# Attention steps of a two-layer diffusion step: the exponential read twice out of PSUM in place of a copy

## What is computed

```python
def one(qblk):
    s = jnp.einsum('bqhd,bkhd->bhqk', qblk, k, preferred_element_type=F32) * scale
    p = jax.nn.softmax(s, axis=-1).astype(v.dtype)
    return jnp.einsum('bhqk,bkhd->bqhd', p, v)
```

## Time and profile before

| | |
|---|---|
| median of 3 runs | 3153.99 us (3151.72 to 3156.88) |
| profiled execution: time | 3155.11 us |
| profiled execution: span from first to last instruction | 3153.0 us |
| mean granted TensorE clock over the span | 0.968 of full |
| PE busy in the span | 3011.7 us, 96% |
| ACT busy, DVE busy, POOL busy | 1001.6 us, 1491.0 us, 904.0 us |

### The profile page before, as it was taken

The page is one execution under the profiler, slowest core; times in us unless marked ns, Lnnn a source line. Parts: engine busy times, 40 slices in busy tenths (PEclk is TensorE's granted clock), DMA queues, the critical chain, the costliest instruction groups (busy, mean ns, idle before and its releaser), DMA issues.

```text
span 3153.0 us, 43418 instructions
## 1 busy us (share of the span) xinstructions
PE 3011.7 (96%) x17065; PEld 2884.9 (91%) x17065; DVE 1491.0 (47%) x1825; ACT 1001.6 (32%) x1439; POOL 904.0 (29%) x573
## 2 busy tenths in 40 slices
PE   7999998999999999888999999998989999999999
PEld 7999998999999999787778888786989999999999
DVE  8445546456445554744566655566442222222222
ACT  3111213111111122323777677776222111121111
POOL 0221121112212121122665556666212112222111
PEclk7999998999999999897999999999989999999999
DMA  5222220222212221120000000000201111111112
GB/s 202 96 80 80 80 100 27 81 80 81 70 61 80 80 73 60 53 82 6 8 7 7 2 7 5 8 7 1 100 27 47 41 40 40 47 40 41 40 45 80
DMA packets 45539, 166.69 MB, mean 53 GB/s; under 512 B 5793, under 2 KB 7457, under 8 KB 45217
## 3 DMA queue, kind: packets, MB, share of 16 engines
q1 hardware_dynamic: 44912, 160.89, 15.0%
q10 hardware_dynamic: 560, 4.87, 0.4%
HBM read 156.15 MB, written 9.58 MB: 53 GB/s over the span
## 4 chain that ended last, share of the span: by engine, by line
PE 53%; issue 30%; POOL 14%; DVE 2%; ACT 1%; POOLq 0%; DVEq 0%; ACTq 0%
PE ps L907 52%; POOL p_lo L505 10%; POOL w_lo L489 2%; DVE x L1466 0%; POOL rot L516 0%; POOL q_tok L520 0%; DVE ps L1382 0%; POOL rot L514 0%; PE ps L1002 0%; PE ps L1212 0%; ACT tmp L592 0%; PE ps L996 0%; DVE tmp L1406 0%; POOLq L504 0%; DVE sums L1801 0%
## 5 line engine op out<-in xcount | busy, mean ns | idle before, releaser
L489 POOL TENSOR_TENSOR w_lo<-w_raw,w_hi 128x1024 fp32r<-128x1024 f32 (+2 forms) x190 | 465.2, 2449 | 1884.3 <-ACT w_hi L585 1884.3
L907 PE MATMUL ps<-h_hi,w_hi 128*128 128x384 f32 x2640 | 606.8, 337 | 37.7 <-DVE h_lo L1447 20.2
L907 PE MATMUL ps<-h_lo,w_hi 128*128 128x384 f32 x2640 | 603.3, 336 | 0.0
L907 PE MATMUL ps<-h_hi,w_lo 128*128 128x384 f32 x2640 | 602.6, 336 | 0.0
L907 PEld LDWEIGHTS ps<-h_hi,w_hi 128*128 128x128 f32 x2640 | 473.7, 190 | 42.4 <-issue 29.8
L585 ACT ACTIVATE w_hi<-w_raw 128x1024 fp32r<-128x1024 f32 (+2 forms) x190 | 194.7, 1025 | 956.7 <-PE ps L907 860.9
L907 PEld LDWEIGHTS ps<-h_lo,w_hi 128*128 128x128 f32 x2640 | 474.3, 189 | 0.0
L907 PEld LDWEIGHTS ps<-h_hi,w_lo 128*128 128x128 f32 x2640 | 473.6, 189 | 0.0
L505 POOL TENSOR_TENSOR p_lo<-p,p_hi 128x512 fp32r<-128x512 f32 (+1 forms) x304 | 389.8, 1294 | 257.2 <-ACT p_hi L830 253.3
L1466 DVE SCALAR_TENSOR_TENSOR x<-ps,mod,x 128x256 f32<-128x256 f32 (+5 forms) x432 | 240.2, 612 | 457.9 <-PE ps L907 456.9
L907 PE MATMUL ps<-hid_hi,w_hi 128*128 128x384 f32 x1536 | 348.8, 334 | 0.5 <-DVE x L1466 0.5
(11 more groups left out here) (142 smaller groups left out, 3551.4 us busy)
## 6 DMA issues: line engine op xcount, KB each, us to landing
w_raw<-in_wall_dram SPq DMA_DIRECT2D x174, 512.0 KB, 3.7
mod_raw<-in_mod_rows_dram SPq DMA_DIRECT2D x80, 512.0 KB, 3.6
x<-in_x_t_dram SPq DMA_DIRECT2D x8, 576.0 KB, 8.4
x_spill<-x ACTq DMA_DIRECT2D x1, 4608.0 KB, 13.8
x<-x_spill SPq DMA_DIRECT2D x1, 4608.0 KB, 13.5
out_dram<-x SPq DMA_DIRECT2D x8, 576.0 KB, 2.8
mod_shift<-in_mod_cols_dram SPq DMA_DIRECT2D x8, 512.0 KB, 14.5
mod_scale<-in_scale_rows_dram SPq DMA_DIRECT2D x8, 512.0 KB, 16.6
```

The lines of the kernel that those rows point to most:

```text
L489: pool.tensor_tensor(w_lo[s][:, 0:words], w_raw[s][:, 0:words], w_hi[s][:, 0:words].bitcast(F32), ALU.subtract).then_inc(w_lo_done, 1)
L907: ins = pe.matmul(out, lhs[a], rhs[b](cols), start=first and n == 0, stop=last and n == 2)
```

## The change

In each attention step ACT takes the exponential twice out of the PSUM bank: first into the high part `p_hi` (signal `p_hi_done`), then into `p32` (signal `p_exp`). The copy from `p32` to `p_hi`, and ACT's wait for its own first exponential, are gone. POOL waits for both signals before it subtracts. Nothing else differs; PE still takes `p_exp` as the sign that the bank may be overwritten.

```diff
@@ p_low, POOL
                 pool.wait_ge(p_hi_done, A.count("j", -1))
+                pool.wait_ge(p_exp, A.count("j", -1))
                 pool.tensor_tensor(p_lo[s][:, 0:n], p32[s][:, 0:n], p_hi[s][:, 0:n].bitcast(F32),
                                    ALU.subtract).then_inc(p_lo_done, 1)
@@ step, ACT
                     act.wait_ge(p_free, A.count("j", 1 - PR if pos < 2 else -1))
+                    act.activation(p_hi[s][:, 0:n], bank(3 + pos % 2, n), ACT.Exp, scale=SCALE).then_inc(p_hi_done, 1)
                     act.activation(p32[s][:, 0:n], bank(3 + pos % 2, n), ACT.Exp, scale=SCALE).then_inc(p_exp, 1)
-                    act.wait_ge(p_exp, A.count("j", -1))
-                    act.activation(p_hi[s][:, 0:n], p32[s][:, 0:n], ACT.Copy).then_inc(p_hi_done, 1)
```

## The result

| | before | after |
|---|---|---|
| median of 20 runs each | 3155.4 us | 3158.85 us |
| lowest and highest | 3151.72, 3159.25 us | 3155.89, 3163.41 us |
| ratio, with its 95% interval | | 1.0015 [1.0008, 1.0022] |
| profiled execution: time, span | 3155.11, 3153.0 us | 3157.41, 3155.6 us |
| mean granted clock over the span | 0.968 | 0.969 |

The changed kernel is slower by 2.5 to 6.9 us (the interval times 3155.4). The single times of either kernel lie in two groups some 5 us apart, and the median of before falls between its groups, so the 3.45 us between the medians are known no better than that interval. The forecast was 3157 us in a range of 3150 to 3165 us.

What follows compares the result with a forecast made beforehand. PE, busy 96% of the span, bounds the kernel and waits for ACT's bank in steps 13 to 22; 7 x 0.43 = 3.0 us on 3155.11 gives 3158.1, as a median 3157 us, range 3150 to 3165 us.

Steps and rivals of the forecast that it cites:

- The bank in steps 13 to 22: PE waits for the later bank at S17, S19 and S22, 0.27, 0.33 and 0.85 us late in the second pair.
- The spacing: On ACT, the second exponential starts 0.48 us after the first; upper end 0.59 us.
- the bank in full: Rival: the bank stalls S17, S19, S22, 1.42 us per pair, 3164 us; decides from 0.53 us between exponentials; chance 0.2.
- the walk: Delays followed through the second pair, step 14 to the max tile of step 23: 0.43 us late, 3.0 us over seven pairs.
- The payback: Before the max tile of step 23, two ACT steps each 0.21 us shorter return 0.42 of 0.85 us.
- V15 and POOL: Low part 0.18 us earlier, POOL's second wait free; V15's 0.2 us wait gone, leaving PE 0.07 us late.
- Where it is covered: steps 0 to 12: Steps 0 to 12 and 23 to 35: 1.08 us of slack against a bank given back 0.48 us later.
- the prediction's own signs: Wrong if exponentials start 0.55 us or more apart, max-tile steps wait for the bank, or V13 to V23 isn't longer.
- The low part's pace: Rival: the loop from V over the exponential and low part to V bounds; 18 us faster, 3136 us; chance 0.06.
- The clock: Rival: TensorE's clock falls at pair starts become fewer or more, 5 us less or more; chance 0.12, half each side.
- The last pair: PE waits there for POOL; sooner low part and later bank roughly cancel: zero, with an end of 2.3 us gained.

Runs made afterwards that it cites:

- run 1: The changed kernel with the copy back in steps 15 to 21 alone; median 3151.23 us, ratio 0.9997 to the kernel before.
- run 2: The kernel before with two exponentials in steps 15 to 21 alone, the copy in all others; ratio 1.0032 to the kernel before.
- run 3: The changed kernel with the first output's two copies after step 11 instead of 14; ratio 1.0002 to the kernel before.
- run 7: The changed kernel with ACT's wait for its first exponential put back between the two; 3168.4 us, ratio 1.0044 to the kernel before.
- run 11: The changed kernel with DVE's third piece of the division by the sums moved behind the row maxima; 3146.35 us, ratio 0.998 to the kernel before.
- run 12: The kernel before with only DVE's third piece of the division by the sums moved behind the row maxima; 3139.55 us, ratio 0.9955.
- run 4: The changed kernel with POOL waiting for the second exponential (p_exp) alone; ratio 1.0016 to the kernel before.
- run 5: The kernel before with only the first output's copies after step 11 instead of 14; ratio 1.0004 to the kernel before.
- run 8: The kernel before with the first output's copies after step 11 instead of 14, traced again on another chip; 3159.77 us beside 3151.88 us for before.
- run 9: The changed kernel with the copy in steps 15 to 21 and output after step 11, again on another chip; 3155.94 us, before 3151.88 us.
- run 10: The changed kernel with copy in steps 15 to 21, output after step 11, DVE's third division piece behind the row maxima; 3135.2 us, ratio 0.9944.

## Why the prediction was right, and where not

**The bank in steps 13 to 22: right.** S17, S19 and S22 are late by 0.30, 0.37 and 0.90 us against 0.27, 0.33 and 0.85 us; runs 1 and 2 show that these steps alone make it, run 3 that the output starts it, and run 7 that each of the three adds a further delay of the bank once. A fourth wait, at S21, was not foreseen; it isn't on the way. The spacing, the one number that the trace of before didn't have, came out at 0.49 us (0.48 taken from two copies out of PSUM). Run 7, at 0.63 us, is the rival with the bank in full; it costs 1.2 us per pair, where the walk had 1.42 us at 0.59 us already, because the walk held ACT for twice the spacing.

**The payback: right in place, a little large.** V20 to V23 is shorter by 0.37 us of the 0.42 us, and run 7, which takes the shorter steps away, takes nearly all of it. Together 0.46 us in the pair that was walked instead of 0.43 us. The other pairs lost up to 0.62 us, which one pair couldn't show, so it is 3.7 us for the sum of 3.0 us.

**V15 and POOL: small and mis-sized.** POOL's second wait costs 0.06 us and not nothing, so the low part is 0.12 us earlier and not 0.18 us. Of the forecast gain the shorter spacing was 0.63 - 0.48 = 0.15 us and the shorter read 0.64 - 0.60 = 0.04 us, not half each. The wait of V15 is gone, as said, and V15 is 0.04 us late where the walk had 0.07 us.

**"Where it is covered: steps 0 to 12": this step failed, at S5.** The slack of 1.08 us was read at S7 in the second pair and taken for all steps with max tiles. At S7 most of it is real: in pair one, at the full clock, E5 ends at 1504.46 + 0.58 = 1505.04 us and S7 starts at 1505.94, 0.90 us later. S5, behind the table load, has none there. In pair two it had 1.34 us (E3 ends at 1596.62 + 0.60, S5 starts at 1598.56), and that was slack that the slow matmuls of the lower clock had made. By the prediction's own signs, a wait for the bank in a step with max tiles counts against it. It cost little here, 0.5 us in pair one, because the clock falls in the other six pairs of the changed kernel. At a full clock it brings 2.8 us more, and the change costs 6.8 us (runs 11 and 12).

The Trainium skill, page "PSUM — Partial Sum Buffer", section "Summary: rules for kernel authors", says to "Evacuate promptly", without a price or a place. The traces show a cost of holding a bank at S17, S19 and S22 and, at a full clock, at S5, not in each of 304 steps.

**The rivals.** The bank in full needed 0.53 us between the two and got 0.49 us. The low part's pace wasn't the bound: in the changed kernel no wait of PE for POOL is left in these steps, and with POOL 0.06 us sooner (run 4) V13 to V20 is 0.07 us shorter of 10.77 us. The clock gave and took nothing in sum between the two profiles, by the luck of pairs two and three; V13 to V23 runs at the full clock in both, and there the change costs 0.5 to 0.6 us per pair, in runs 11 and 12 as well. A single profile's total within 2 us isn't a proof of the sum, and the forecast's 3157 us stood on a median of 3 runs that was 1.4 us below that of 20; what is shown is the stretches, and a total of 2.5 to 6.9 us. The last pair, put at zero, is near it: V0 to V37 takes 71.15 us before and 70.87 us after, 70.01 us in run 12 and 70.29 us in run 11.

What stays open: why the lower clock lasts longer in runs 5, 8 and 9, and why pair three of before keeps the full clock behind the same wait. The runs show that the lower clock is gone in runs 10 to 12, where PE's wait of 1.9 us is down to 0.5 us; in runs 5 and 8 the wait itself is 1.9 us as before.

## What to carry to other kernels

Holding a buffer longer costs only where its next writer has less slack than the holding adds, so the price of such a change is found by walking the few steps with little slack; once that is used up, each of them adds a further delay once (0.14 us each in run 7). Take the slack of every wait at the full clock, and at the first step of a stretch as well as in its middle, for slack that is read where the clock has fallen can be the clock's and go when it comes back. And when PE's clock falls in most turns of a loop, first try to remove the wait ahead of the fall: here that was worth 12.9 us, by the stretches more than half of it the wait itself and the rest the clock, while 0.8 us per turn won elsewhere came out as nothing.

## What the runs showed that was not expected

A second semaphore wait in front of a POOL instruction cost 0.06 us though its semaphore had been met half a microsecond before (0.14 against 0.08 us). An exponential out of PSUM behind another of the same bank started 0.49 us after it and each lasted 0.60 us, so they overlap by 0.11 us; with a wait on the first one's end between them it is 0.63 us. And a gain of 5.6 us in the steps of the attention was gone in the total, with TensorE granted 0.965 instead of 0.968 of its clock over the span; in the profile that shows it best, run 8, the seven stretches from S3 to V13 are 8.2 us longer than before, and 10.6 us longer than in the other profile of the same kernel.
